# q and k of two layers transposed in 32x32 squares by VectorE and moved by ScalarE, instead of on TensorE

## The reference

```python
# fox: 16 heads of 128
q, k, v, gate, f_logit = split(x @ w_in)
q, k = rms_norm(heads(q), q_gain), rms_norm(heads(k), k_gain)
c = cumsum(log_sigmoid(f_logit + b_f))
s = q @ k.T * 128**-0.5 + c[:, None] - c[None, :]        # causal
y = softmax(s) @ v * silu(gate)
h = layer_norm(ALPHA * x + y @ w_out)
# ret: 8 heads of 256 (q, k) and 512 (v)
q, k = rotary(q), rotary(k) * 256**-0.5
o = (q @ k.T * decay) @ v                                # decay per head, causal
y = group_norm_heads(o) * silu(gate)
out = layer_norm(ALPHA * h + y @ w_out)
```

## Time and profile before

| | |
|---|---|
| Runs | 2329.92 us median of 3 (2329.48 to 2330.32) |
| Span of the profiled execution, first to last instruction | 2326.9 us |
| Its own time | not listed apart; the runs' median is 3.0 us above the span |
| TensorE busy | 2314.0 us (99%) |
| VectorE busy | 1571.4 us (68%) |
| ScalarE busy | 1132.5 us (49%) |
| Mean granted TensorE clock | 0.999 |
| The four fox v blocks end, gate blocks begin (us in the span) | about 1160.8, 1257.2, 1375.4, 1494.0 |

### The profile page before, as it was taken

How to read it: one execution, slowest core, us unless ns; L and a number is a source line. 1 busy time by engine, 2 the same in 40 slices (tenths; PEclk the granted TensorE clock), 3 DMA queues, 4 the chain that set the end, 5 groups by cost and what they waited for, 6 DMA issues and landing times.

```text
span 2326.9 us, 31382 instructions
## 1 busy us (share of the span) xinstructions
PE 2314.0 (99%) x11420; PEld 1947.7 (84%) x11420; DVE 1571.4 (68%) x2019; ACT 1132.5 (49%) x1404; POOL 48.7 (2%) x60
## 2 busy tenths in 40 slices
PE   9999999999999999999999999999999999999998
PEld 8788888888888888888888888888888888888886
DVE  6687576966777777668656666687656556456567
ACT  6444555554554555544454544456444434444443
POOL 1000000000000000000100000000000000000000
PEclk9999999999999999999999999999999999999999
DMA  9566546666666666665699659955655655655644
GB/s 314 154 182 209 169 151 187 190 189 192 190 188 191 191 187 193 190 194 181 215 175 188 181 173 168 186 189 174 197 174 178 192 173 173 201 186 164 198 159 177
DMA packets 220782, 434.06 MB, mean 187 GB/s; under 512 B 13456, under 2 KB 13744, under 8 KB 219904
## 3 DMA queue, kind: packets, MB, share of 16 engines
q1 hardware_dynamic: 218704, 422.50, 62.9%
q0 software_dynamic: 1536, 9.75, 1.2%
q10 hardware_dynamic: 432, 0.30, 0.0%
HBM read 430.30 MB, written 2.11 MB: 186 GB/s over the span
## 4 chain that ended last, share of the span: by engine, by line
PE 98%; issue 1%; DVE 1%; POOL 0%; DVEq 0%; ACT 0%; POOLq 0%
PE acc L558 77%; PE mix L558 19%; PE mix L653 0%; PE mix L731 0%; PE mix L1023 0%; PE mix L1049 0%; PE mix L747 0%; DVE res L2481 0%; DVEq L145 0%; DVE table L1961 0%; POOL rstd L497 0%; POOL arena L475 0%; DVE w_lo L1653 0%; DVE res L2306 0%; DVE res L1675 0%
## 5 line engine op out<-in xcount | busy, mean ns | idle before, releaser
L1653 DVE TENSOR_TENSOR w_lo<-raw,w_hi 128x1024 fp32r<-128x1024 f32 x787 | 959.9, 1223 | 553.7 <-ACT w_hi L1132 547.9
L1132 ACT ACTIVATE w_hi<-raw 128x1024 fp32r<-128x1024 f32 (+1 forms) x793 | 836.7, 1057 | 835.3 <-PE acc L558 646.1
L558 PE MATMUL acc<-w_hi,x_both 128*128 128x512 f32 x2784 | 891.0, 394 | 0.0
L558 PEld LDWEIGHTS acc<-w_hi,x_both 128*128 128x128 f32 x2784 | 522.7, 188 | 107.6 <-DVE x_both L2318 0.3
L558 PE MATMUL acc<-w_lo,x_both 128*128 128x512 f32 x1392 | 542.0, 389 | 0.0
L558 PE MATMUL acc<-x_both,w_hi 128*128 128x512 f32 (+2 forms) x1216 | 410.0, 389 | 0.4 <-DVE z L1972 0.4
L558 PE MATMUL acc<-x_both,w_lo 128*128 128x256 f32 x1168 | 316.9, 280 | 0.0
L558 PEld LDWEIGHTS acc<-w_lo,x_both 128*128 128x128 f32 x1392 | 261.7, 188 | 52.1
L558 PE MATMUL mix<-x_both,w_hi 128*128 128x512 f32 x768 | 267.0, 394 | 0.0
L558 PEld LDWEIGHTS acc<-x_both,w_hi 128*128 128x128 f32 (+1 forms) x1216 | 223.6, 186 | 48.9 <-issue 0.8
L558 PE MATMUL acc<-w_hi,y_hi 128*128 128x512 f32 x640 | 252.7, 395 | 0.0
(11 more groups left out here) (231 smaller groups left out, 1498.9 us busy)
## 6 DMA issues: line engine op xcount, KB each, us to landing
raw<-in_ret_w_in SPq DMA_DIRECT2D x192, 512.0 KB, 4.0
raw<-in_w_up SPq DMA_DIRECT2D x176, 512.0 KB, 4.3
raw<-in_fox_w_in SPq DMA_DIRECT2D x128, 512.0 KB, 5.3
raw<-in_w_down SPq DMA_DIRECT2D x88, 512.0 KB, 3.7
raw<-in_w_in SPq DMA_DIRECT2D x78, 512.0 KB, 3.7
raw<-in_ret_w_out SPq DMA_DIRECT2D x64, 512.0 KB, 3.7
raw<-in_w_out SPq DMA_DIRECT2D x32, 512.0 KB, 3.7
raw<-in_fox_w_out SPq DMA_DIRECT2D x32, 512.0 KB, 4.1
```

Of the source, the lines that this page charges most:

```text
L558: return nc.tensor.matmul(o, l, r, start=start, stop=stop)
L1132: return nc.scalar.activation(o, i_, f, **kw)
L1653: V.tensor_tensor(lo, raw[:, g.base % RAW, :], hi, ALU.subtract).then_inc(lo_done, 1)
```

## The change

T and E of the fox heads and T and its copies of the ret heads are gone. VectorE now transposes the whole `qk` of a group, one instruction for each token tile of 128x1024, in independent 32x32 squares, into a free buffer (`spare` in fox, `rp` in ret). ScalarE then moves the squares to their place, back into the memory of `qk` (now viewed as `qkT`): an instruction takes 32 source partitions (quarter a) to 32 target partitions (quarter b).

- fox: the transpose of a token tile stands right behind its normalising multiplication, with a wait between them, in slots 21 and 22. 32 moves of 32 partitions x 256 elements, 4 in each of the slots 23 to 30; half of them carry the gain as a scale. The first waits for both transposes (`turned`). Slot 23's four stand ahead of the drain of v.
- ret: transposes in slots 26 and 28, 16 moves of 32 x 512 elements, 2 in each of the slots 29 to 36.
- S reads `qkT` and waits for `moved`. In ret, S takes over T's wait for all blocks, and O of a second head waits for `r_t`.
- The product of the two fox gains is formed at the start (`G_FOX4`), so only q's squares are scaled.

```diff
             def att_step(A, what, n, h, group, blk0):
                 if what == "T":
+                    if A is fox:
+                        return
...
-                    pe.wait_ge(A.qk_sb, n.at(1))
+                    if A is fox:
+                        pe.wait_ge(A.moved, group.at(1))
+                    else:
+                        pe.wait_ge(A.qk_sb, n.at(1))
+                    q, k = (qkT[:, h, :], qkT[:, GROUP + h, :]) if A is fox else (qT[:, 0, :], kT[:, 0, :])
...
-                if what == "T":
+                if what == "S":
                     if h == 0:
                         all_out(pe, blk0)
-                    pe.wait_ge(r_rot, group.at(1))
...
+                    pe.wait_ge(r_moved, group.at(1))
...
+            def move(turned, moved, n, squares, s, per, each):
+                for k in range(s * per, min((s + 1) * per, 16 * each)):
+                    if k == 0:
+                        act.wait_ge(turned, n.at(1, TOK))
+                    x, b, a = k % each, k // each % 4, k // each // 4
+                    w = 8 // each
+                    out = qkT[QUAD * b:QUAD * (b + 1), w * x:w * (x + 1), :]\
+                        .rearrange("p g (t a c) -> p t a g c", t=TOK, a=4)[:, :, a]
+                    src = squares[QUAD * a:QUAD * (a + 1), :, w * x:w * (x + 1), b, :]
+                    scale = gains[QUAD * a:QUAD * (a + 1), G_FOX4 + b:G_FOX4 + b + 1]
+                    done = a_(out, src, ACT.Copy, **({"scale": scale} if each == 2 and x == 0 else {}))
+                    if k == 16 * each - 1:
+                        done.then_inc(moved, 1)
...
+                    if TURN_AT <= s < TURN_AT + 8:
+                        move(fox.turned, fox.moved, group, fox_turned, s - TURN_AT, 4, 2)
...
+                    if RET_TURN_AT <= s < RET_TURN_AT + 8:
+                        move(r_turned, r_moved, group, ret_turned, s - RET_TURN_AT, 2, 1)
...
-            slots(g.plus(25), 7, none)
+            slots(g.plus(25), 7, fox_move(Count(0)), 24)
...
-                    if part == 3:
+                    if A is fox:
+                        link(done)
+                        V.transpose(fox_turned[:, t].rearrange("p g b c -> p (g b c)"),
+                                    qk[:, t, :, :].rearrange("p h c -> p (h c)")).then_inc(fox.turned, 1)
+                    elif part == 3:
                         done.then_inc(A.normed, 1)
...
+                    if s in (26, 28):
+                        t = (s - 26) // 2
+                        V.transpose(ret_turned[:, t].rearrange("p g b c -> p (g b c)"),
+                                    qk[:, t, :, :].rearrange("p h c -> p (h c)")).then_inc(r_turned, 1)
```

More of the change, by code:

```diff
@@ L69 @@
 V_LO_AT = 25
+TURN_AT, RET_TURN_AT = 23, 29
+QUAD = 32
 OUT_PARTS = ((0, 0, D // 2), (0, D // 2, D // 2), (1, 0, D // 2), (1, D // 2, COL), (1, 3 * COL, COL))
@@ L235, in mixers_kernel, with squares_of @@
         rp = arena[:, 4096:6144]
+        qkT = qk[:].rearrange("p t h c -> p (t h c)").rearrange("p (g s) -> p g s", g=8)
+        def squares_of(buffer):
+            return buffer.rearrange("p (t g b c) -> p t g b c", t=TOK, g=8, b=P // QUAD)
+        fox_turned, ret_turned = squares_of(spare), squares_of(rp)
         def rounded(name, at, *shape):
@@ L250, in mixers_kernel @@
         G_FFN, G_POOL, G_Q, G_K, G_FQ, G_FK, G_LG, G_LB = 0, 16, 24, 25, 26, 27, 28, 44
-        VECTORS = 60
+        G_FOX4 = 60
+        VECTORS = 68
         raw_full = [sem(f"raw_full{k}") for k in range(RAW)]
@@ L296, in __init__ @@
                 self.masked, self.inverse = sem(p + "masked"), sem(p + "inverse")
-                self.qk_mm, self.qk_sb = sem(p + "qk_mm"), sem(p + "qk_sb")
+                if p == "fox_":
+                    self.turned, self.moved = sem(p + "turned"), sem(p + "moved")
+                else:
+                    self.normed, self.qk_mm, self.qk_sb = (sem(p + n) for n in ("normed", "qk_mm", "qk_sb"))
                 self.biased = sem(p + "biased")
@@ L307, in mixers_kernel @@
         dec_full, ln_full = sem("dec_full"), sem("ln_full")
-        r_qk_mm, r_qk_sb, r_s_mm, r_st, r_o_mm = (sem("r_" + n) for n in ("qk_mm", "qk_sb", "s_mm", "st", "o_mm"))
+        r_turned, r_moved, r_s_mm, r_st, r_o_mm = (sem("r_" + n) for n in ("turned", "moved", "s_mm", "st", "o_mm"))
         r_v_lo, r_s_parts = sem("r_v_lo"), sem("r_s_parts")
@@ L738, in att_step @@
                         o = M[1][:, t * P:(1 + 2 * t) * P]
-                        done = mm(o, qT[:, 0, t * P:(t + 1) * P], kT[:, 0, 0:(t + 1) * P], True, True)
+                        done = mm(o, q[:, t * P:(t + 1) * P], k[:, 0:(t + 1) * P], True, True)
                     done.then_inc(A.s_mm, 1)
@@ L1011, in ret_step @@
             def ret_step(what, n, h, group, blk0):
-                if what == "T":
+                if what == "S":
                     if h == 0:
                         all_out(pe, blk0)
-                    pe.wait_ge(r_rot, group.at(1))
[L1016 to L1026, removed]
+                    pe.wait_ge(r_moved, group.at(1))
                     if h > 0:
                         pe.wait_ge(r_lo, n.at())
+                    q, k = qkT[:, 2 * h:2 * h + 2, :], qkT[:, 4 + 2 * h:6 + 2 * h, :]
                     for dt in range(2):
-                        mm(M[2][:, 0:S], kT[:, dt, 0:P], qT[:, dt, :], dt == 0, dt == 1)
+                        mm(M[2][:, 0:S], k[:, dt, 0:P], q[:, dt, :], dt == 0, dt == 1)
                     for dt in range(2):
-                        done = mm(M[2][:, S:S + P], kT[:, dt, P:S], qT[:, dt, P:S], dt == 0, dt == 1)
+                        done = mm(M[2][:, S:S + P], k[:, dt, P:S], q[:, dt, P:S], dt == 0, dt == 1)
                     done.then_inc(r_s_mm, 1)
@@ L1036, in ret_step @@
                     pe.wait_ge(r_v_lo, n.at(1))
+                    if h > 0:
+                        pe.wait_ge(r_t, n.at())
                     for c, bank, t in ((0, 0, 0), (1, 1, 0), (2, 1, 1)):
@@ L1050, in ret_step @@
                     done.then_inc(r_y_mm, 1)
-            RET_AT = {0: "T", 2: "S", 4: "O", 7: "Y"}
+            RET_AT = {2: "S", 4: "O", 7: "Y"}
             def ret_slots(n, group, blk0, stride=RET_STRIDE):
@@ L1258, in step @@
                         m, r = n.plus(h), s - stride * h
-                        if r in (0, 2, 3):
+                        if r in ((2, 3) if gated else (0, 2, 3)):
                             att_step(A, {0: "E", 2: "P", 3: "C"}[r], m, h, gq, gk)
@@ L1263, in step, with fox_move, ret_move, both @@
                             a_(y_hi[:, y0 + h, :], y_att if gated else M[3][:, 0:S], ACT.Copy).then_inc(A.y_hi, 1)
+                return step
+            def move(turned, moved, n, squares, s, per, each):
[11 more added lines that the diff above has]
+                        done.then_inc(moved, 1)
+            def fox_move(group):
+                def step(s):
+                    if TURN_AT <= s < TURN_AT + 8:
+                        move(fox.turned, fox.moved, group, fox_turned, s - TURN_AT, 4, 2)
+                return step
+            def ret_move(group):
+                def step(s):
+                    if RET_TURN_AT <= s < RET_TURN_AT + 8:
+                        move(r_turned, r_moved, group, ret_turned, s - RET_TURN_AT, 2, 1)
+                return step
+            def both(one, two):
+                def step(s):
+                    one(s)
+                    two(s)
                 return step
@@ L1503, in _ @@
             for b in range(1, 3):
-                slots(g.plus(1 + 8 * b), 8, forget, 8 * b)
+                slots(g.plus(1 + 8 * b), 8, both(forget, fox_move(Count(0))), 8 * b)
                 drain(g.plus(9 + 8 * b), Count(FOX_B + 1 + b), b)
-            slots(g.plus(25), 7, none)
+            slots(g.plus(25), 7, fox_move(Count(0)), 24)
             gate_low(g.plus(33), Count(FOX_B + 4), 0, 0)
@@ L1515, in fox_group @@
                 blk = Count(FOX_B + 6 - 9, 9, i)
-                step = att_slots(fox, Count(-4, 4, i), G_FQ, G_FK, 0, True)
+                step = both(att_slots(fox, Count(-4, 4, i), G_FQ, G_FK, 0, True), fox_move(Count(0, 1, i)))
                 slots(g, 8, step)
-                drain(g.plus(8), blk, 0, [(fox.normed, i)])
+                drain(g.plus(8), blk, 0, [(fox.turned, i * TOK)])
                 slots(g.plus(8), 8, step, 8)
@@ L1522, in fox_group @@
                 drain(g.plus(24), blk.plus(2), 2, [(fox.y_mm, i * 4)])
-                slots(g.plus(24), 7, none)
+                slots(g.plus(24), 7, fox_move(Count(0, 1, i)), 24)
                 act.wait_ge(fox.y_sb, 4 * i)
@@ L1557, in step @@
                     m = n.plus(h)
[L1558 to L1564, removed]
+                    if r == 6:
                         act.wait_ge(r_t, m.at(1))
@@ L1582, in _ @@
             for b in range(1, 6):
-                slots(g.plus(8 * b), 8, none, 8 * b)
+                slots(g.plus(8 * b), 8, ret_move(Count(0)), 8 * b)
```

(13 more changed lines are left out.)

1 line of the change is left out of this document (removed).

## The result

The changed kernel takes 2339.36 us (median of 4 runs, 2338.71 to 2341.32) against 2329.98 (2329.48 to 2330.32): ratio 1.0042, 95% interval [1.0029, 1.0054]. It is 9.4 us slower, twice the 0.2% of the prediction's bound. The forecast was 2332 with a range of 2325 to 2342. The range held, but the case that came was not the one held likeliest: it was rival 1, the clock.

The account below looks back on a forecast made before the run. TensorE, busy 2314.0 of 2326.9 us, was taken as the bound. Removed transposes (-14.0) and four fox pauses (+16.0) gave +2.0, so 2329.9 became 2331.9, rounded to 2332; own range 2328 to 2334.6, wide range 2325 to 2342.

Parts of the forecast that it names:

- the prediction's bound: Whole kernel: a change within 0.2% (4.7 us) counts as the same time; this outcome had chance 0.45.
- rival 1: Fox pauses: TensorE's clock falls to 1.2 GHz, 1.9 us each, 7.6 for four, 2339.5 us; chance 0.30 for the clock.
- The removed transposes: TensorE, fox and ret heads: 0.44 us for each of 16 and 0.87 for each of 8, together 14.0 saved.
- Ret adds nothing: Ret slots: the added transposes and moves fit into idle time of VectorE and ScalarE, at a cost of 0.
- The four pauses: Fox gate blocks: TensorE waits for the drain of v behind transposes and moves, 3 x 3.76 + 4.77 = 16.0 us.
- four pauses with no fall of the clock or with one: Fox gate blocks: the forecast's case, 2332 us, or 2334 with one clock fall; chance 0.45.
- Cover in the slots from 24 on: ScalarE in fox: four moves of 1.38 us beside a split of 0.97 fit into a slot of 2.8.
- Rival 3: Whole kernel: nothing is late and the gain stands, 2315.9 us, 0.6% faster; chance 0.12 in whole or large part.

Follow-up runs that it names:

- ret alone: The kernel before with only the ret half of the change: 2322.69 us against 2329.89, ratio 0.9969.
- experiment 10: The changed kernel with 16 extra 128x128 identity matmuls on TensorE inside each fox pause, results unused: 2332.66 us, ratio 1.0011 to the kernel before.
- experiment 4: The changed kernel with one fox move instead of four in slot 23, ahead of the drain of v: 2334.52 us, ratio 1.0020 to the kernel before.
- Experiments 6: The changed kernel with all fox moves behind the drain of v, and fox groups 1 and 3 reading the weight columns of groups 0 and 2: 2316.08 us.
- 11: The kernel called drains first, with fox heads of groups 0 and 2 put back to T on TensorE: 2319.75 us, ratio 0.9956 to the kernel before.
- drains first: The kernel called moves behind the drain, with v drained before slot 23's last split and slot 30's moves put behind the gate's second half drain: 2322.08 us.
- moves behind the drain: The changed kernel with fox moves starting in slot 24 instead of 23, all behind the drain of v: 2324.41 us, ratio 0.9976 to the kernel before.
- experiment 9: The changed kernel with 40 extra 128x128 identity matmuls on TensorE inside each fox pause, results unused: 2350.92 us, ratio 1.0092 to the kernel before.

## Why the prediction came out as it did

- *The removed transposes* were put at 14.0 us. Ret measured 7.2 against 7.0; with 14.5 (clock 6.7) to 15 (clock 7.2) for both, fox has 7.3 to 7.8 against 7.0. Right in mechanism; the size of the fox part is what the sum leaves over.
- *Ret adds nothing*: right; ret alone has no new wait.
- *The four pauses* stood at the forecast places, with the forecast releaser. 16.0 was forecast, 17.2 came. The transposes take 1.24 against 1.22. The moves were sized too small: with a scale 0.506 and without 0.398 long, but 0.41 apart each, so the four take 1.65 and not 1.38; that is the 0.3 us in each pause.
- *The step that failed* is the weighing of rival 1. The forecast's case was "four pauses with no fall of the clock or with one". The clock fell in all four. With the clock held up the kernel takes 2332.66 (experiment 10), near the forecast's 2332: the misses in the pauses (1.2 more) and in the transposes (0.5 to 1.0 more) nearly cancel there, and the clock is what is left. The row that pointed to it was read: the clock down 3.7 us after the last matmul. Against pauses of 3.8 and 4.8 this should have been the likeliest case. One row also gives no spread: in the four pauses the delay was 2.0 to 4.5 us, and experiment 4 has a fall behind an idle time of 2.60.
- *Luck in the rival's number.* Its price for the clock, 7.6, came close to 6.7 (experiment 10) and 7.2 (windows), but it rested on the assumption that the low clock lasts as long as the pause, which no row showed; behind the pauses TensorE worked 2.9 to 5.2 us at it. That the rival's 2339.5 is the measured time is luck too: the pauses were 1.2 us longer, the transposes worth more and the clock cost less than forecast, and these errors cancel.
- The statement on the clock taken from the Trainium skill (TensorE: Matmul & The Clock Gate, Why this matters for your kernels), that pauses between matmuls bring it down, is borne out by the windows at 0.50. The advice of the Trainium skill (VectorE: DVE Perf Modes, Rules for kernel authors) to transpose 128x128 on TensorE is not borne out where TensorE is the bound and ScalarE has the time for the moves: in ret the squares gain 7.2 us, and in fox the change as made lost by the place of the moves.
- *Cover in the slots from 24 on*: put at 0.97 + 1.38 in 2.8. It was 2.72 of 2.77. In the changed kernel this was harmless; once the pauses were gone it showed.
- *Rival 3* ("the gain stands, 2315.9") took for granted that each T taken from TensorE counts. Experiments 6 and 11 show that half of the fox heads stand where the weights bind as soon as TensorE is faster. The same oversight was in the prediction's claim that all of the 14.0 us lie on the path. The DMA shares of the kernel before would have shown it; I did not read them.
- Not tried: the same moves with a fifth raw buffer, and anything that tells why the addresses of groups 1 and 3 are slow. That they are is shown; the reason is open.

## What to carry to other kernels

Where an engine is the bound and its neighbours have time to spare, ask not only how much work is moved to them but in front of what it is queued. Here four short copies that wait stood ahead of a drain with 0.1 us to spare; the pauses from that, 17.2 us, were more than the 15 that all removed transposes gave. A pause of the bounding engine is to be priced twice, once for its length and once for the clock behind it. And before a gain on the bounding engine is counted in full, read what the next resource (here the DMA share of each stretch) has left there.

## What the runs showed of the hardware that was not expected

- The same amount of weights, in transfers of the same size, comes at a DMA share of 1.02 from one set of columns (169 GB/s, drains first) and of 0.59 from another (170 GB/s, moves behind the drain).
- Behind a wait of 2.60 us the clock was at 1.2 GHz, behind one of 3.10 it stayed at 2.4, in one and the same execution (experiment 4). In the changed kernel it fell 2.0 to 4.5 us after the last matmul had ended, and TensorE then worked at it for 2.9 to 5.2 us.
- A copy on ScalarE of 32 partitions x 256 without a scale is 0.398 long and one with a scale 0.506, but each is followed by the next after 0.41.
- A transpose of 128x1024 fp32 on VectorE takes 1.24 us, as long as the multiplication of that size ahead of it (1.23). A 128x128 fp32 matmul of the identity is shown as two instructions and takes 0.22 us (experiment 9), where a transpose of the same size takes 0.09.
